# A bias over distances filled in stretches by Pool, and sparse attention's branches added by Pool

## The reference

```python
return gc[..., 0:1] * o_c + gc[..., 1:2] * o_s + gc[..., 2:3] * o_w
```

```python
d = jnp.maximum(dist, 0)
large = max_exact + (jnp.log(df / max_exact) / math.log(REL_MAX_DIST / max_exact)
                     * (REL_BUCKETS - max_exact)).astype(jnp.int32)
large = jnp.minimum(large, REL_BUCKETS - 1)
return jnp.where(d < max_exact, d, large)
```

## Time and profile before

| | |
|---|---|
| runs | 1242.01, 1246.18, 1246.53 us |
| profiled execution | 1245.61 us, its span 1243.9 us |
| mean granted clock of PE | 0.994 of full speed |
| busy: PE, DVE, ACT, POOL | 1214.9, 567.9, 388.1, 33.5 us |
| instructions: PE, DVE, ACT, POOL | 6088, 882, 611, 63 |

### The profile page before, as it was taken

How to read it: one execution, slowest core, us unless ns; L and a number is a source line. 1 busy time by engine, 2 the same in 40 slices (tenths; PEclk the granted TensorE clock), 3 DMA queues, 4 the chain that set the end, 5 groups by cost and what they waited for, 6 DMA issues and landing times.

```text
span 1243.9 us, 15474 instructions
## 1 busy us (share of the span) xinstructions
PE 1214.9 (98%) x6088; PEld 1011.9 (81%) x6088; DVE 567.9 (46%) x882; ACT 388.1 (31%) x611; POOL 33.5 (3%) x63
## 2 busy tenths in 40 slices
PE   7999999999999999999999999999999999999997
PEld 7788888888887888997877888887788888888886
DVE  3444444432226445336788534564544444442224
ACT  4322222221115212236544222333522222221113
POOL 0100000000002100000020000000000000000000
PEclk8999999999999999999999999999999999999999
DMA  6573333332234333462200032323233333323211
GB/s 182 156 230 100 85 88 98 101 119 102 102 101 129 100 104 100 136 203 69 71 3 2 1 102 70 116 102 102 68 102 91 85 94 101 101 101 119 102 68 68
DMA packets 137967, 123.52 MB, mean 99 GB/s; under 512 B 4116, under 2 KB 125116, under 8 KB 137868
## 3 DMA queue, kind: packets, MB, share of 16 engines
q1 hardware_dynamic: 133664, 108.02, 28.2%
q0 software_dynamic: 4144, 14.83, 3.8%
q10 hardware_dynamic: 112, 0.03, 0.0%
HBM read 118.42 MB, written 8.90 MB: 102 GB/s over the span
## 4 chain that ended last, share of the span: by engine, by line
PE 91%; DVE 5%; ACT 2%; DMA 1%; issue 1%; SPq 0%; ACTq 0%; DVEq 0%
PE ps L1248 54%; PE ps L1327 18%; PE ps L1412 4%; PE ps L1507 3%; PE ps L1646 3%; PE ps L1466 2%; PE ps L1630 2%; PE ps L1477 2%; DVE x_tok L849 1%; DVE y_gained L843 1%; PE ps L1618 1%; DMA x_tok<-in_x 1%; PE ps L1272 1%; DVE pT_sb L1038 1%; ACT ring_hi L593 1%
## 5 line engine op out<-in xcount | busy, mean ns | idle before, releaser
L1248 PE MATMUL ps<-xn_hi,ring_hi 128*128 128x512 f32 x992 | 388.4, 391 | 1.8 <-DVE xn_lo L833 1.8
L1248 PE MATMUL ps<-xn_hi,ring_lo 128*128 128x512 f32 x992 | 386.2, 389 | 0.0
L1248 PE MATMUL ps<-xn_lo,ring_hi 128*128 128x512 f32 x992 | 386.0, 389 | 0.0
L808 DVE TENSOR_TENSOR ring_lo<-ring_raw,ring_hi 128x2048 fp32r<-128x2048 f32 (+1 forms) x89 | 201.8, 2268 | 249.1 <-ACT ring_hi L583 249.1
L583 ACT ACTIVATE ring_hi<-ring_raw 128x2048 fp32r<-128x2048 f32 (+1 forms) x89 | 167.9, 1887 | 258.4 <-PE ps L1327 157.6
L1248 PEld LDWEIGHTS ps<-xn_hi,ring_hi 128*128 128x128 f32 x992 | 186.3, 188 | 41.6 <-issue 4.0
L1248 PEld LDWEIGHTS ps<-xn_hi,ring_lo 128*128 128x128 f32 x992 | 186.2, 188 | 39.1
L1248 PEld LDWEIGHTS ps<-xn_lo,ring_hi 128*128 128x128 f32 x992 | 186.3, 188 | 38.0
L1327 PE MATMUL ps<-ring_hi,hT_hi 128*128 128x512 f32 x352 | 136.9, 389 | 0.0
L1327 PE MATMUL ps<-ring_hi,hT_lo 128*128 128x512 f32 x352 | 136.9, 389 | 0.0
L1327 PE MATMUL ps<-ring_lo,hT_hi 128*128 128x512 f32 x352 | 136.9, 389 | 0.0
(11 more groups left out here) (228 smaller groups left out, 1132.5 us busy)
## 6 DMA issues: line engine op xcount, KB each, us to landing
ring_raw<-in_ffn_w_gu SPq DMA_DIRECT2D x88, 512.0 KB, 4.9
ring_raw<-in_ffn_w_down SPq DMA_DIRECT2D x44, 512.0 KB, 3.6
ring_raw<-in_w_in SPq DMA_DIRECT2D x44, 512.0 KB, 4.5
ring_raw<-in_w_out SPq DMA_DIRECT2D x8, 512.0 KB, 3.7
bias_rows_sparse<-bias_by_distance POOLq DMA_DIRECT2D x1, 2560.0 KB, 13.3
x_tok<-in_x SPq DMA_DIRECT2D x4, 512.0 KB, 5.6
ring_raw<-in_cmp_w_k SPq DMA_DIRECT2D x4, 512.0 KB, 4.4
ring_raw<-in_cmp_w_v SPq DMA_DIRECT2D x4, 512.0 KB, 7.1
```

Source lines behind the costliest of these rows:

```text
L808: e = dve.tensor_tensor(dst, src, f32(r), ALU.subtract)
L1248: e = pe.matmul(ps[:, 2 * (slot if pair is None else pair) + c, :], part(a, slot, k * 256 + c * P, P), xn[b][:, k, :], start=(k == 0 and i ...
```

## The change

Two things. First, the bias: the 0/1 matrix is gone, as are PE's five products, ACT's five copies and the 33rd row. The host hands over rel_bias transposed, so that each of 20 partitions (heads) holds its 32 buckets. Pool fills bias_vec with the masking number, changes the sign of the table, and then copies, for each stretch of equal buckets, one element spread over the stretch: 107 stretches (28, 28, 23, 16 and 12 in the five areas), 1298 elements. The store and the replication after it stand as they were. DVE's wait for the store stands too.

Second, the additions into y_nsa: take_half on DVE ends with the scaling into o_tmp, and Pool makes the additions (add_half), placed among its transfers and its products on o_dil. From the second pair on, DVE waits for Pool's additions of the same half of the pair before, ahead of writing o_tmp. PE's transposes of y_nsa, and DVE's gate step 4, wait for all of Pool's additions. The memset on w_n that carried y_nsa_ready is gone.

```diff
+def bucket_runs():
...
+    of = bucket(dist)
+    runs = []
+    for first, end, step in ((NSA_AT, CMP_AT, 1), (CMP_AT, D0_AT, 1), (D0_AT, D1_AT, 1), (D1_AT, D2_AT, 1), (D2_AT, TAB_W, 4)):
+        at = [int(j) for j in i[first:end] if keep[j]]
+        for b, group in itertools.groupby(at, key=lambda j: int(of[j])):
+            group = list(group)
+            assert group == list(range(group[0], group[0] + step * len(group), step))
+            runs.append((b, group[0], step, len(group)))
+    return runs
...
-            pool.dma_start(tab[0:BUCKETS, :], rel).then_inc(small_loaded, 16)
-            pool.dma_start(onehot_sb[0:BUCKETS + 1, :], onehot).then_inc(small_loaded, 16)
+            pool.dma_start(tab[0:20, :], rel).then_inc(small_loaded, 16)
+            pool.memset(bias_vec[0:20, :], MASKED).then_inc(vec_filled, 1)
...
-            pool.wait_ge(vec_copied, 5)
+            pool.wait_ge(small_loaded, 16)
+            pool.tensor_scalar(neg_tab[0:20, :], tab[0:20, :], -1.0, None, ALU.mult).then_inc(tab_negated, 1)
+            pool.wait_ge(tab_negated, 1)
+            pool.wait_ge(vec_filled, 1)
+            for b, first, step, n in RUNS:
+                e = pool.tensor_copy(bias_vec[0:20, first:first + step * (n - 1) + 1:step], neg_tab[0:20, b:b + 1].broadcast_to([20, n]))
+            e.then_inc(vec_filled, 1)
+            pool.wait_ge(vec_filled, 2)
             pool.dma_start(vec_dram, bias_vec[0:20, :]).then_inc(vec_stored, 16)
...
+            def add_half(pair, half):
+                pool.wait_ge(o_nsa_read, 2 * pair + half + 1)
+                for b in range(2):
+                    if half:
+                        y = y_nsa[:, 0:NT:2, pair::HPG, :].rearrange("p t h d -> p h t d")
+                        o = o_tmp[:, half, :].rearrange("p (b h t d) -> p b h t d", b=2, h=2, d=HD)[:, b]
+                        e = pool.tensor_tensor(y, y, o, ALU.add)
+                    else:
+                        y = y_nsa[:, 3, pair::HPG, :]
+                        pool.tensor_tensor(y, y, heads2(o_tmp[:, half, 128 * b:128 * b + 128]), ALU.add)
+                        y = y_nsa[:, 1, pair::HPG, :]
+                        o = o_tmp[:, half, 256:512].rearrange("p (h b d) -> p b h d", h=2, d=HD)[:, b]
+                        e = pool.tensor_tensor(y, y, o, ALU.add)
+                    e.then_inc(branch_added, 1)
+                    pool.wait_ge(branch_added, 4 * pair + 2 * half + b + 1)
...
+            pool.wait_ge(yc_ready, NT)
+            add_half(0, 0)
             pool.wait_ge(c_ready, 1)
...
+            add_half(0, 1)
             pool.wait_ge(c_loaded, 16)
             pool.wait_ge(o_read, NDU)
...
+            for pair in range(1, HPG):
+                for half in range(2):
+                    add_half(pair, half)
             pool.wait_ge(gates_scaled, NGATE)
...
-                    for c in BIAS_PARTS[u] if p == 0 else ():
-                        act.wait_ge(vec_mm, c + 1)
-                        act.activation(bias_vec[0:20, c * S:c * S + S], ps[0:20, BIAS_BANKS[c], :], ACT.Copy,
-                                       scale=-1.0).then_inc(vec_copied, 1)
...
+                if pair:
+                    dve.wait_ge(branch_added, 4 * (pair - 1) + 2 * half + 2)
                 dve.tensor_tensor(heads2(o_tmp[:, half, :]), heads2(ps[:, 6 + half, :]),
                                   f.unsqueeze(2).broadcast_to([P, 8, HD]), ALU.mult).then_inc(o_nsa_read, 1)
-                dve.wait_ge(o_nsa_read, 2 * pair + half + 1)
-                for b in range(2):
-                    if half:
...
-                        chain(dve.tensor_tensor(y, y, o, ALU.add))
...
-                    if p == 0:
-
-                        pe.wait_ge(small_loaded, 32)
-                        pe.wait_ge(tab_ready, 1)
-                        for c in BIAS_PARTS[u]:
-                            if c >= 3:
-                                pe.wait_ge(vec_copied, c - 2)
-                            pe.matmul(ps[0:20, BIAS_BANKS[c], :], tab[0:BUCKETS + 1, :], onehot_sb[0:BUCKETS + 1, c * S:c * S + S],
-                                      start=True, stop=True).then_inc(vec_mm, 1)
...
             pe.wait_ge(yd_summed, 6)
-            pe.wait_ge(y_nsa_ready, 1)
+            pe.wait_ge(branch_added, 4 * HPG)
```

More of the change, by code:

```diff
@@ L21 @@
+import itertools
 import math
@@ L71 @@
 assert TAB_W == 5 * S
-BIAS_PARTS = ((0, 1), (2, 3, 4))
-BIAS_BANKS = (4, 5, 6, 4, 5)
 CMP_ZERO = CB - 1 + CS * (CPAD - 1)
@@ L101, in bucket @@
     return np.where(d < exact, d, np.minimum(large, BUCKETS - 1))
-def bucket_table():
+def bucket_runs():
     i = np.arange(TAB_W)
@@ L158, in layer_kernel @@
                  pos_v, cw1_v, cw2_v, w_bn, w_bd, w_out, gm_post, g2_pre, w2_gu, w2_down, g2_post,
-                 rel, onehot, out):
+                 rel, out):
     DIL, CMP, NSA = units()
+    RUNS = bucket_runs()
     NDU, NNU = len(DIL), len(NSA)
@@ L189, in layer_kernel @@
     gains_row = at("gains_row", R + 16 * K, [P])
-    onehot_sb = at("onehot_sb", R + 56 * K, [TAB_W])
     bias_vec = at("bias_vec", R + 68 * K, [TAB_W])
@@ L268, in layer_kernel @@
     rstd = small("rstd", [NT])
-    tab = small("tab", [20])
+    tab = small("tab", [BUCKETS])
+    neg_tab = small("neg_tab", [BUCKETS])
     posT = small("posT", [2, 16])
@@ L300, in layer_kernel @@
     small_loaded, gains_loaded, x_sums = sem("small_loaded"), sem("gains_loaded"), sem("x_sums")
-    consts, vec_mm, vec_copied, vec_stored = sem("consts"), sem("vec_mm"), sem("vec_copied"), sem("vec_stored")
-    tab_ready, rows_stored = sem("tab_ready"), sem("rows_stored")
+    consts, vec_filled, vec_stored = sem("consts"), sem("vec_filled"), sem("vec_stored")
+    tab_negated, rows_stored = sem("tab_negated"), sem("rows_stored")
     xT_done = sem("xT_done")
@@ L322, in layer_kernel @@
     yc_ready = sem("yc_ready")
+    branch_added = sem("branch_added")
     stats_stored, stats_loaded, e_in, e_ready, c_ready, c_stored, c_loaded = (
@@ L332, in layer_kernel @@
         sem("odil_scaled"), sem("ydT_done"), sem("yd_summed"), sem("ydhi_ready"), sem("ydlo_ready"))
-    y_nsa_ready, ynT_done, ynhi_ready, ynlo_ready = sem("y_nsa_ready"), sem("ynT_done"), sem("ynhi_ready"), sem("ynlo_ready")
+    ynT_done, ynhi_ready, ynlo_ready = sem("ynT_done"), sem("ynhi_ready"), sem("ynlo_ready")
     b_done, b_gated, a_done, a_gated, merged, mhi_ready, mlo_ready = (
@@ L906, in ffn @@
                 add_y(p)
-            dve.memset(tab[BUCKETS:BUCKETS + 1, :], -MASKED).then_inc(tab_ready, 1)
             dve.wait_ge(cT_gains, 1)
@@ L1079, in take_half @@
                 dve.wait_ge(pv_done, u1)
+                if pair:
+                    dve.wait_ge(branch_added, 4 * (pair - 1) + 2 * half + 2)
                 dve.tensor_tensor(heads2(o_tmp[:, half, :]), heads2(ps[:, 6 + half, :]),
                                   f.unsqueeze(2).broadcast_to([P, 8, HD]), ALU.mult).then_inc(o_nsa_read, 1)
-                dve.wait_ge(o_nsa_read, 2 * pair + half + 1)
-                for b in range(2):
-                    if half:
-                        y = y_nsa[:, 0:NT:2, pair::HPG, :].rearrange("p t h d -> p h t d")
-                        o = o_tmp[:, half, :].rearrange("p (b h t d) -> p b h t d", b=2, h=2, d=HD)[:, b]
-                        chain(dve.tensor_tensor(y, y, o, ALU.add))
[L1088 to L1093, removed]
             def dil_weights():
@@ L1165, in _ @@
                     take_half((i - 13) // 10, 1)
-            e = dve.memset(w_n[:, :, :], 0.0)
-            e.then_inc(y_nsa_ready, 1)
-            dve.wait_ge(y_nsa_ready, 1)
             for i in range(NGATE):
@@ L1172, in _ @@
                 dve.wait_ge(w_used, n + 1)
+                if i == 4:
+                    dve.wait_ge(branch_added, 4 * HPG)
                 for c in range(2):
@@ L1348, in ffn @@
                 pe.wait_ge(hlo_ready, h0 + UP - 2)
-                if p == 0:
-                    pe.wait_ge(vec_copied, 5)
                 for n in range(DOWN - 1):
@@ L1668 @@
         a = np.ascontiguousarray(inputs[name])
-        if name != "rel_bias":
-            a = a[0]
+        a = np.ascontiguousarray(a.T) if name == "rel_bias" else a[0]
         arrays[f"in_{name}"] = a
-    arrays["bucket_of_distance"] = bucket_table()
     for name, a in arrays.items():
```

## The result

The changed kernel takes 1231.66 us (median of four runs, 1231.50 to 1231.74) against 1245.53 us (four runs): ratio 0.9894, 95% interval 0.9878 to 0.9909. It was forecast at 1237.2 with a range of 1232.5 to 1241.5. The direction was right; the gain is 13.9 us instead of 9.0, and the time lies 0.8 us under the range. The same kernel once more, beside later experiments, took 1231.57 us (ratio 0.9894, 0.9877 to 0.9910).

What follows compares the result with a forecast made beforehand. PE, busy 98%, was taken to bound the kernel. Start 1.5 + bias matmuls 4.5 + additions 4.0 - collision 1.0 = 9.0 us off the profiled 1245.61; 1236.6, as a median 1237.2, range 1232.5 to 1241.5.

Steps and rivals of the forecast that it cites:

- The bias matmuls: PE's queue after steps 0 and 1: removing both groups of products gains 4.5 us, bounds 4.2 to 4.7.
- The start: Before step 0: without the 0/1 table's load x_tok lands sooner, gaining 1.5 us, bounds 0 and 3.5.
- a rival at 0.13: Clock at the start: x_tok early enough avoids the clock's fall, transposes shrink by up to 2 us more: 1235.2 or 1234.2.
- The late next: Before step 0: low half of the first weights ready about 17.0 us against PE's 18.2, so not in the way.
- The filling: Pool's 107 bias copies at 140 ns each plus 1.7 ns an element, ending at 25.6 us; no engine waits for it.
- The collision: Replication beside weight loads, before step 2 or 3: 1.0 us lost, bounds 0 and 3.7; full meeting a rival, chance 0.15, 1239.9.
- The additions: Sparse attention: moving them from DVE to Pool ends PE's waits, gaining 4.0 us, bounds 0 and 4.3.
- The port rule: Pool's filling beside DVE's differences of weight halves: the two exclude each other, Pool waits; sum the same within 0.3 us.

Runs made afterwards that it cites:

- run 9: Changed kernel with five unread products of the old bias shape back in PE's queue, after steps 0 and 1: 1238.58 us, ratio 0.9939.
- run 1: Kernel before, with Pool's load of the 0/1 table issued only after the first weights landed: 1242.56 us against 1245.28, ratio 0.9979.
- run 2: Changed kernel plus an unused load of 33 rows of 10 KB at the start: 1235.18 us; first group 1233.7 to 1235.3, second 1240.4 to 1243.6.
- run 7: Changed kernel plus the load of 33 rows of 10 KB, with the replication held until PE is past step 2: 1234.62 us, ratio 0.9916.
- run 8: Changed kernel, replication held until PE is past step 2, plus the same 0.34 MB load spread over 128 partitions: 1232.78 us, ratio 0.9896.
- run 3: Kernel before, with 19 more products on the identity while PE waits for x_tok, to keep the clock up: 1244.54 us against 1245.28, ratio 0.9997.
- run 10: Changed kernel, replication held until PE is past step 2, first weights loaded in two halves of k: 1230.74 us, ratio 0.9893.
- run 11: The changed kernel itself, unedited, measured again on a later occasion: 1231.57 us.
- run 6: Changed kernel with 57 of Pool's 107 bias copies, so the replication starts earlier: 1238.15 us, ratio 0.9930.
- run 5: Changed kernel with the five replicating transfers held until PE is past step 2: 1233.27 us, ratio 0.9897.

## Why the prediction was wrong, step by step

- **The bias matmuls: right, a little small.** 4.5 us from the chain, at most 4.7; 4.84 in the starts of the steps, 4.86 in run 9. The chain counts the products and leaves out the slower matmuls around them, which the same text had counted in the attention.
- **The start: the step that failed.** "I take 1.5 us" came from a tenth of the transfers' bytes. It was 4.45 us between the profiled executions (4.70 in run 1's) and about 3 in the medians (2.7 in run 1, 3.1 by the first group of run 2). The bound of 3.5 holds for the medians and not for the profiles. Two things were mis-sized. First the landing: x_tok's last part came 3.5 us earlier (12.43 to 8.97), not 1.5. The bytes were spread as if evenly, though the text itself said that the rows are few and large: put back as rows they move the landing to 11.1 and 11.4 us (runs 7 and 2), in smaller pieces to 9.4 (run 8), and the profiles without any such load have 8.6 to 9.3. Second the clock, which was left to a rival at 0.13, worth up to 2 us: with x_tok early PE idled 1.1 us instead of 4.5, kept its clock, and its transposes took 2.5 us less (5.33 to 2.81). Both come from the same landing and belong in one term, though how much of the gain is the clock's alone run 3 could not tell. Nor is the fall certain from the wait: in run 9 PE idled 2.0 us before x_tok and its clock fell, in run 10 it idled 2.3 us and it did not.
- **The late next: named, but said not to be in the way.** The low half of the first weights was put at about 17.0 us against PE's 18.2. It was ready at 14.9, and PE, through with its own work earlier still, waited 1.27 us for it. Of the 5.96 us by which the products on the identity began earlier (17.71 to 11.75) this gave 1.5 back.
- **The filling: right in kind and nearly in size, from other parts.** It began at 8.7 and ended at 27.0: 18.3 us, 17.2 forecast. Three long copies (below) hold 4.3 us more than their neighbours, which the text had seen as possible and left out of its sum. The starts of the others lie 122 ns apart in the median, where 140 was taken, and an element costs about 0.9 ns (278 ns for 118 elements against 175 for one), where 1.7 was taken.
- **The collision: right in mechanism, the size of one execution.** 1.0 us was taken, 0.35 measured, between bounds of 0 and 3.7, and nothing in run 11's profile. The load that the text watched, that of step 3, just escaped (4.5 us); that of step 4, issued at 32 us, was hit: its second half took 24.3. The bound was too low: fully met, the collision costs 4 to 5 us of waiting and then the clock, 7 to 8 us in all in the profiles of runs 6 and 2. And the miss at the start carries over. For a replication from 25.0 us the text had the load of step 3 landing at 49.9 and a wait of 0.7; in run 6 it began at 24.28 and the load landed at 49.7, as forecast, but PE, 3.6 us ahead by the earlier start, was due at step 3 at 49.7 and not 53.4. Less 4.2 us for the halves it needed the load by 45.5, and waited 4.1.
- **The additions: right.** 4.26 us, 4.0 taken; PE has no wait left from 624 to 684 us. DVE never waited for Pool. Pool's price was too low: the text took 606 against 425 ns, 1.4 times DVE's, from a product on other tiles; the additions themselves took 734 and 461 ns against 425 and 292, 1.7 and 1.6 times. It did not matter, as nobody waits for them.
- **The port rule: the trace agrees.** The copies have a median of 178 ns and a longest of 2248 ns. Three of the 107 are long, 1.2, 1.3 and 2.2 us (started at 13.73, 16.45 and 22.91), and they are those that meet DVE's differences of 1.23, 1.22 and 2.29 us (started at 13.70, 16.47 and 22.82), as the Trainium skill ("SBUF — State Buffer", Who interferes with whom) has it. No other copy took over 0.28 us. DVE's differences were not longer than before.

```profile
L510 POOL COPY bias_vec<-neg_tab x107: 175/178/2248, 8.7 to 26.8; 20x1 f32<-20x1 f32 x57, 20x2 f32<-20x2 f32 x5, 20x8 f32<-20x8 f32 x4, 20x6 f32<-20x6 f32 x4
```

- The rest of the miss is the fall of the clock at the start of attention (0.9 us in the profile of before, none after). It comes with the change and without it, and the prediction did not know the term. What decides whether the clock falls there was not tried.

The sum with the measured terms is 4.45 + 4.84 + 4.26 - 0.35 + 0.9 = 14.1 us, the difference of the profiled spans. In the medians, 13.9 us apart, the start and all falls of the clock together have 13.9 - 4.84 - 4.26 + 0.35 = 5.1 us. Some 3 of them are the start; how the rest divides is open. Most runs of the kernel before beside the experiments have a mean clock of 0.993 to 0.995, the eight of the changed kernel 0.996 to 0.998.

## What to carry to other kernels

A load that nobody waits for can still be on the path: what it is beside at the start decides, and here its form (few large rows on the software queue) counted more than its bytes. When a transfer's lateness leaves PE idle and its clock can fall, price the wait and the clock as one term. When a large background transfer moves, write down which load is issued in the few microseconds around its new start, by PE's new times and not the old ones: taking copies off Pool made this kernel slower. One wait that places the transfer can take that chance away; none of the sixteen runs with such a wait (runs 5, 7, 8 and 10) took over 1235.9 us.

## What was not expected of the hardware

- A software-queue transfer of 5.25 MB in pieces of mostly 4 to 5 KB leaves the weights' loads (pieces of 512 bytes) little: the second 512 KB of a load took 22.7 to 25.0 us beside it (24.27 in the changed kernel, 25.04 in run 2, 24.20 in run 6, 22.7 in run 11), against 4 to 6 us with nothing beside it.
- The same 0.34 MB delayed x_tok's last part to 11.1 us as 33 rows (run 7) and to 9.4 us in 64 pieces (run 8); without such a load it was there at 8.6 to 9.3, so the second delay is hardly one.
- Pool's additions of 256 elements took 734 ns (611 for the product on o_dil of the same size), those of 128 elements 461, against DVE's 425 and 292.

```profile
L564 POOL TENSOR_TENSOR y_nsa<-y_nsa,o_tmp 128x256 f32<-128x256 f32 x8 | 5.9, 734 | 24.1 <-DVE o_tmp L1111 23.8
L567 POOL TENSOR_TENSOR y_nsa<-y_nsa,o_tmp 128x128 f32<-128x128 f32 x8 | 3.7, 461 | 49.4 <-DVE o_tmp L1111 49.0
```
